# The first four projection units of layer 0 on unnormed x, two of them side by side

## What is computed

```python
def rms_norm(x, g):
    y = xf * lax.rsqrt(jnp.mean(xf * xf, axis=-1, keepdims=True) + NORM_EPS)
    return y * g

h = rms_norm(x, norm_g)
proj = jnp.einsum('bsd,de->bse', h, w_in) + b_in
(a_q, a_k, a_v, i_q, i_k, i_w, ...) = jnp.split(proj, offsets, axis=-1)
a_k = partial_rope(a_k, cos, sin);  i_q = partial_rope(i_q, ...);  i_k = partial_rope(i_k, ...)
logits = jnp.einsum('bqhd,bsd->bqhs', iqb, ik)                     # indexer
score = jnp.einsum('bqhs,bqh->bqs', jax.nn.relu(logits), iwb)      # then top 128 of each row
...
x = x + jnp.einsum('bsd,de->bse', merged, w_out)
```

## Time and profile before

| | before |
|---|---|
| median of 3 runs | 1283.41 us |
| the profiled execution's own time | 1283.52 us |
| its span (first to last instruction) | 1281.3 us |
| PE busy | 1263.1 us, 99% |
| DVE, ACT, POOL busy | 689.0, 633.3, 599.5 us |
| granted TensorE clock | 0.999 of full |

### The profile page before, as it was taken

The page is one execution under the profiler, slowest core; times in us unless marked ns, Lnnn a source line. Parts: engine busy times, 40 slices in busy tenths (PEclk is TensorE's granted clock), DMA queues, the critical chain, the costliest instruction groups (busy, mean ns, idle before and its releaser), DMA issues.

```text
span 1281.3 us, 19785 instructions
## 1 busy us (share of the span) xinstructions
PE 1263.1 (99%) x6486; PEld 1064.3 (83%) x6486; DVE 689.0 (54%) x1432; ACT 633.3 (49%) x1157; POOL 599.5 (47%) x759
## 2 busy tenths in 40 slices
PE   8999999999999999999999999999999999999997
PEld 6788888888988888888888888878888888888887
DVE  6799887745545221123687988785644631121144
ACT  6565676686534332333256466767754433323233
POOL 6654333423235555455775642333322455455463
PEclk9999999999999999999999999999999999999999
DMA  7223111221322323333342321122212222332331
GB/s 296 83 82 115 67 50 58 66 91 51 113 69 70 103 82 98 99 97 108 99 158 89 99 85 65 50 66 73 76 51 102 89 82 82 106 98 90 103 102 66
DMA packets 37047, 116.35 MB, mean 91 GB/s; under 512 B 4080, under 2 KB 4464, under 8 KB 36720
## 3 DMA queue, kind: packets, MB, share of 16 engines
q1 hardware_dynamic: 34672, 111.24, 26.3%
q10 hardware_dynamic: 2304, 4.20, 1.0%
HBM read 111.23 MB, written 4.19 MB: 90 GB/s over the span
## 4 chain that ended last, share of the span: by engine, by line
PE 92%; DVE 4%; ACT 2%; issue 1%; POOL 1%; DMA 0%; ACTq 0%; SPq 0%; DVEq 0%; POOLq 0%
PE acc L653 75%; PE ps_o L812 5%; PE ps_t L799 2%; PE ps_t L790 2%; PE ps_s L768 2%; PE ps_o L819 1%; PE ps_s L774 1%; DVE turn L1371 1%; DVE bk_lo_s L1351 1%; PE ps_s L757 1%; PE acc L686 1%; PE spare L750 1%; PE spare L831 1%; DVE prob L1392 0%; DMA xT<-x 0%
## 5 line engine op out<-in xcount | busy, mean ns | idle before, releaser
L604 POOL TENSOR_TENSOR w_lo<-w_raw,w_hi 128x256 fp32r<-128x256 f32 x744 | 586.0, 817 | 664.2 <-ACT w_hi L889 664.0
L653 PE MATMUL acc<-h_hi,w_hi 128*128 128x512 f32 x1120 | 447.6, 400 | 0.7 <-POOL h_lo L615 0.7
L653 PE MATMUL acc<-h_lo,w_hi 128*128 128x512 f32 x1120 | 438.8, 392 | 0.0
L653 PE MATMUL acc<-h_hi,w_lo 128*128 128x512 f32 x1120 | 292.6, 395 | 0.0
L889 ACT ACTIVATE w_hi<-w_raw 128x1024 fp32r<-128x1024 f32 (+1 forms) x210 | 202.0, 962 | 119.5 <-PE acc L653 90.8
L653 PEld LDWEIGHTS acc<-h_hi,w_hi 128*128 128x128 f32 x1120 | 210.7, 188 | 41.7 <-POOL h_lo L615 1.8
L653 PEld LDWEIGHTS acc<-h_lo,w_hi 128*128 128x128 f32 x1120 | 210.7, 188 | 39.4
L653 PEld LDWEIGHTS acc<-h_hi,w_lo 128*128 128x128 f32 x1120 | 205.6, 188 | 40.4
L1513 DVE SCALAR_TENSOR_TENSOR gated<-prob,acc 128x512 f32<-128x512 f32 x16 | 11.0, 688 | 246.7 <-PE acc L653 246.7
L1131 ACT ACTIVATE prob<-acc,par_half 128x512 f32<-128x512 f32 x48 | 33.1, 690 | 147.1 <-PE acc L653 147.1
L1078 ACT ACTIVATE prob<-prob,neg_max 128x128 f32<-128x128 f32 (+3 forms) x128 | 70.7, 553 | 9.2 <-DVE neg_max L1392 8.9
(11 more groups left out here) (274 smaller groups left out, 1823.0 us busy)
## 6 DMA issues: line engine op xcount, KB each, us to landing
w_raw<-w_full SPq DMA_DIRECT2D x162, 512.0 KB, 3.4
w_raw<-w_mix SPq DMA_DIRECT2D x48, 256.0 KB, 2.6
rel<-rel ACTq DMA_DIRECT2D x16, 256.0 KB, 2.9
xT<-x SPq DMA_DIRECT2D x4, 512.0 KB, 6.2
stage<-x_tok SPq DMA_DIRECT2D x4, 512.0 KB, 10.1
xT<-x SPq DMA_DIRECT2D x1, 2048.0 KB, 9.3
x_kept<-xT SPq DMA_DIRECT2D x1, 2048.0 KB, 9.0
xT<-x_kept SPq DMA_DIRECT2D x1, 2048.0 KB, 8.3
```

Of the source, the lines that this page charges most:

```text
L604: last = pool.tensor_tensor(w_lo[:, slot, part, :], w_raw[:, raw, part, :], w_hi[:, slot, part, :].bitcast(F32), ALU.subtract)
L653: last = pe.matmul(acc[slot][:, :], w[:, slot, k, :], x[:, k, :], start=(place == 0), stop=(place == 3 * nk - 1))
```

## The change

In layer 0 a fourth unit (a_k) runs on unnormed x, and DVE scales it in a step of its own, `scale_ak`, ahead of the first rotation. Units 0 and 1 are no longer computed one after the other: their first 16 passes are dealt in turns as the chunks of x arrive, so that weights 1 are loaded between the second and the third pair of chunks, and ACT takes their high part there. On ACT the square root and the parameter copies stand in front of the reading of unit 0. The parameters are loaded in front of the last token tile. POOL splits the weights of units 2 and 3 ahead of its first `h_lo`, and those of unit 4 ahead of its third. In both layers `turn_iw` moves from unit 6 into unit 7, ahead of `turn_v`.

```diff
+RAW_X = (4, 3)
@@ schedule(l)
     if l == 0:
-        seq.extend((("passes", (0, 0, PASSES)), ("squares", 0), ("read", 0), ("norm_sum", 0), ("high", 2)))
-        seq.extend((("passes", (1, 0, SPREAD)), ("norm_spread", 0), ("passes", (1, SPREAD, PASSES)), ("h", 0), ("h", 1), ("unit", 1)))
+        seq.extend((("passes", (0, 0, DC)), ("passes", (1, 0, DC))))
+        for k in range(DC, 2 * DC, 2):
+            seq.extend((("passes", (0, k, k + 2)), ("passes", (1, k, k + 2))))
+        seq.extend((("passes", (0, 2 * DC, PASSES)), ("squares", 0), ("norm_sum", 0), ("read", 0), ("high", 2)))
+        seq.extend((("passes", (1, 2 * DC, PASSES)), ("norm_spread", 0), ("unit", 1)))
         seq.append(("passes", (2, 0, PASSES)))
-        seq.extend(("h", c) for c in range(2, DC))
+        seq.extend(("h", c) for c in range(4))
         seq.append(("unit", 2))
+        seq.extend(("h", c) for c in range(4, DC))
...
     seq.extend((("passes", (3, 0, PASSES)), ("unit", 3)))
+    if l == 0:
+        seq.append(("scale_ak", 0))
     seq.extend(("rope", u) for u in range(XG_UNITS))
...
-    seq.append(("turn_iw", 0))
     seq.extend((("iq_hi", 1), ("ik_hi", 0), ("iq_lo", 0), ("iq_lo", 1), ("ik_lo", 0)))
     units(6, 7)
-    seq.append(("turn_v", U_AV))
+    seq.extend((("turn_iw", 0), CUT, ("turn_v", U_AV)))
     index(1)
@@ sync, layer 0
                     load(l, 0, 0, full(0), DC)
-                    for c in range(2, DC, 2):
-                        load_x(c)
+                    load_x(2)
                     load(l, 1, 1, full(1), DC)
+                    load_x(4)
+                    load_x(6)
...
+                    load_params()
                     load_tokens(3)
-                    load_params()
@@ gpsimd
-                for u in range(3):
+                done = 5 if l == 0 else 4
+                for u in range(done - 1):
                     split(l, u, u, DC)
                 for c in range(1, DC, 2):
-                    if c == (3 if l == 0 else 5):
-                        split(l, 3, 3, DC)
+                    if c == 5:
+                        split(l, done - 1, done - 1, DC)
                     pool.wait_ge(h_hi_ready, l * DC + c + 1)
                     pool.tensor_tensor(h_lo[:, c, :], h_full[c % 4], ...).then_inc(h_odd, 1)
@@ scalar, start
-                if c == 1:
-                    high_part(0, 0, 0, 0)
-            high_part(0, 0, 0, 1)
+                if c % 2 and c < 4:
+                    high_part(0, 0, 0, c // 2)
@@ scalar, read_sums
-                    if n < XG_UNITS:
+                    if n < RAW_X[l]:
-                        act.activation(iq[:, n, :] if n < U_IK else ik[:, :], src, ACT.Copy).then_inc(evac, 1)
+                        act.activation(iq[:, n, :] if n < U_IK else ik[:, :] if n == U_IK else ak[:, :], src, ACT.Copy).then_inc(evac, 1)
@@ vector
+                    elif kind == "scale_ak":
+                        dve.wait_ge(evac, evacs(l, U_AK))
+                        link(dve.tensor_tensor(ak[:, :], ak[:, :], spare[:, :], ALU.mult))
+                        link(dve.tensor_scalar(ak[:, :], ak[:, :], par[:, U_AK:U_AK + 1], None, ALU.add))
```

More of the change, by code:

```diff
@@ L64 @@
 K_ID, K_CHUNK, K_CAUSAL, K_COS, K_SIN, KCOLS, K_SEL = 0, 128, 256, 384, 896, 1408, 1408
-SPREAD = 16
 INDEX_AT = {U_AK + 7: 2, U_AK + 12: 3}
@@ L608, in _ @@
             for l in range(DEPTH):
-                for u in range(3):
+                done = 5 if l == 0 else 4
+                for u in range(done - 1):
                     split(l, u, u, DC)
                 for c in range(1, DC, 2):
-                    if c == (3 if l == 0 else 5):
-                        split(l, 3, 3, DC)
+                    if c == 5:
+                        split(l, done - 1, done - 1, DC)
                     pool.wait_ge(h_hi_ready, l * DC + c + 1)
                     pool.tensor_tensor(h_lo[:, c, :], h_full[c % 4], h_hi[:, c, :].bitcast(F32), ALU.subtract).then_inc(h_odd, 1)
-                with pool.Fori(0, (PROJ - 4) // RAW) as i:
-                    for b in range(4, RAW + 4):
+                with pool.Fori(0, (PROJ - done) // RAW) as i:
+                    for b in range(done, RAW + done):
                         split(l, i * RAW + b, b, DC)
-                for u in range(4 + (PROJ - 4) // RAW * RAW, PROJ):
+                for u in range(done + (PROJ - done) // RAW * RAW, PROJ):
                     split(l, u, u, DC)
@@ L728, in _ @@
                         n, first, to = n
-                        product(l, n, n, 0, h_hi if n >= XG_UNITS else xg_hi, h_lo if n >= XG_UNITS else xg_lo, DC, first, to,
+                        product(l, n, n, 0, h_hi if n >= RAW_X[l] else xg_hi, h_lo if n >= RAW_X[l] else xg_lo, DC, first, to,
                                 (lambda k: pe.wait_ge(xg_ready, l * DC + k + 1)) if n == 0 else
-                                (lambda k: pe.wait_ge((h_even, h_odd)[k % 2], l * (DC // 2) + k // 2 + 1)) if n == XG_UNITS else None)
+                                (lambda k: pe.wait_ge((h_even, h_odd)[k % 2], l * (DC // 2) + k // 2 + 1)) if n == RAW_X[l] else None)
                     elif kind == "norm_sum":
@@ L1249, in _ @@
             for l in range(DEPTH):
-                base[0] = l * DVE_STEPS + PRE
+                base[0] = l * (DVE_STEPS + 2)
                 count[0] = 0
@@ L1501, in _ @@
                             last.then_inc(normed, 1)
-                assert count[0] == DVE_STEPS, count[0]
+                assert count[0] == DVE_STEPS + (2 if l == 0 else 0), count[0]
                 hold(dve, "dve")
```

## The result

The changed kernel takes **1288.38 us** (1287.21 to 1288.64) against 1283.41 for the kernel before: a ratio of 1.0035, 95% interval 1.0026 to 1.0045. It is slower by 5.0 us, and above the range of the prediction (1282.6 to 1287.2). Its profiled execution took 1288.64 us (before 1283.52), with a span of 1286.7 (before 1281.3).

What follows compares the result with a forecast made beforehand. PE, busy 99% of the span, was taken as the bound. Terms -1.45 - 1.5 + 1.0 + 3.85 - 0.1 = +1.8 on the profiled 1283.52 gave 1285.3; with the median 0.11 lower, 1285.2 us, range 1282.6 to 1287.2.

Steps and rivals of the forecast that it cites:

- Loads, units 0 and 1: Start of layer 0: weights 1 land at 9.3, PE's stream holds from 11.48, unit 2 starts at 21.9, 1.45 us gained.
- lock-out for a whole GpSimd instruction: Chunks 4 to 7 beside POOL's split: 1.54 each, PE loses 1.5 more, 1286.7; 0.04 of rival 2's chance.
- Rival 3: Loads at the start don't land in issue order, weights 1 as late as before: +3.4, 1286.9; chance 0.06.
- Units 2 to 4: Unit 3's 1.5 of waiting goes, unit 4 loses about 1.0 waiting for `h_lo`; unit 5 starts at 39.4, 1.9 ahead.
- Start of the rotations: DVE in layer 0: after the h chain and `scale_ak`, the first rotation starts at 35.75 against 32.11.
- rival 2: POOL's slower splits delay `h_lo` 1 and DVE's chain; `iw` read at 57.4, +3.3 less 0.1, 1286.7; chance 0.24.
- I take 16.1, since POOL is idle at their end: DVE's three rotations in layer 0 take 16.1 us instead of 16.5, ending at 51.85.
- The low parts: DVE behind the rotations in layer 0: `iq_lo` falls from 3.24 to 2.4, `ik_lo` takes 1.38; `iw` done at 56.05.
- the lag goes to the end whole: Behind `turn_v`, which starts 1.9 late after a 4 us stand, index scores and scans keep their distances to the end.
- Layer 1: DVE does the low parts while formerly waiting 3.37 for `turn_iw`; PE gains 0.1 at the index score at most.

Runs made afterwards that it cites:

- Experiment 7: Changed kernel with GpSimd computing only a quarter of the low parts of the weights of units 5, 6 and 7 in layer 0: 1283.19 us.
- Experiments 1: Changed kernel with twenty passes into an unused score bank added in front of `turn_v` in layer 0: 1285.57 us.
- 3: Changed kernel, layer 0: DVE reads `iw` right behind the rotations; 7 unused passes before `turn_v`, 14 before the first index score: 1285.15 us.
- experiment 4: Kernel before the change, with only the move of `turn_iw` behind unit 6, in front of `turn_v`, in both layers: 1283.32 us.
- experiments 2: Changed kernel with DVE in layer 0 reading `iw` right behind the rotations, in front of `iq_lo`; PE's order unchanged: 1286.27 us.

## Why the prediction was wrong

The sign and the place were right, the size was not: +1.8 forecast, +5.0 measured. By its steps:

- **Loads, units 0 and 1.** Right. Weights 1 land at 2.66 + 6.6 = 9.3 us, as forecast. The stream runs from 11.55 (11.48 forecast) and chunk 7 is used at 16.28 (16.06 to 16.1). Beside the split a chunk took 4.74 / 4 = 1.19, inside 1.15 to 1.2. (The row at 28.24 behind that price lay beside a split for its first half only and then beside POOL's own `h_lo`; the price held all the same.) The Trainium skill's lock-out for a whole GpSimd instruction ("Who interferes with whom") would have made it 1.54, and the measurement decides against that. Unit 2 starts at 21.80 (21.9): 1.57 gained, 1.45 forecast. Rival 3 falls with it.
- **Units 2 to 4.** Right. Unit 4 starts at 33.00 (32.95) and unit 5 at 39.30 (39.4). The wait for `h_lo` is there, 0.86 in two pieces (6.30 for a unit of 5.44; 1.0 forecast).
- **Start of the rotations.** Right in the sum, 35.72 for 35.75, and partly by luck: the chain of h ended at 33.75, so that `scale_ak` could start some 0.4 earlier than forecast, and its addition took 1.14 where 0.5 to 0.86 were put down. `h_lo` 1 ended at 29.4 (29.5), so rival 2 in its own form (two slow splits ahead of it) did not happen, though its time for the reading of `iw`, 57.4, is nearly the measured one.
- **"I take 16.1, since POOL is idle at their end".** This is the first step that failed. The rotations took 17.7. I had looked only at their end, and there it came true: the last product with `turn` took 0.70 for 1.03. But the first one took 1.04 for 0.70, and so gave it back. And the splits moved by 3.4 us where these rotations moved by 3.8 to 4.2 (units 1 and 2). So three `TENSOR_SCALAR` instructions that had started in GpSimd's gaps, two of them only 0.2 to 0.3 ahead of a split, now lie beside one: all five take 4.27 for 3.10, which is the 17.67 - 16.49. Experiment 7 shows the cause by taking GpSimd away. The Trainium skill (SBUF — State Buffer, "Who interferes with whom", "Which ops grab the shared pair") names `tensor_scalar` among the instructions that can contend with GpSimd; the rows agree, 0.97 against 0.49. I had used that page for another step and not here. The low parts took 2.27 (2.4), and `iw` was released near 57.3 instead of 56.05, **+1.25**.
- **"the lag goes to the end whole".** The second step that failed, by leaving a term out. I counted a stand of PE at its length. TensorE's granted clock fell, and the eleven starts behind it were nearly twice as far apart: **+2.5**. Experiments 1 and 3 show it. I had read PE's distances only where PE hardly stood, and taken 0.23 a pass for all of it.
- **Layer 1.** 0.3 came back, 0.1 forecast.

With both put right the sum closes: 1.8 + 1.3 + 2.5 - 0.2 = 5.4, the difference of the spans; the profiled executions themselves differ by 5.1, since 0.3 less lies around the span of after.

What stays open: what decides in one execution whether the clock falls. In the profiles slow starts followed the stands of 2.15, 2.82, 3.26 and 5.17, and none the stands of 1.44, 1.99, 2.14 and 2.74; and experiment 4 shows them behind waits of 0.85, 0.41 and 0.41. So the length of the stand does not settle it. The times say that it differs from one execution to the next: in experiments 2 and 7, and in the changed kernel itself, where two of seven times are 1287.2 and 1287.3 with a mean clock of 0.997 and 0.996, and the others 1288.1 to 1288.6 with 0.995. No experiment varied the work in front of a stand.

## What to carry to other kernels

A gain at the front of the critical engine is worth what is left of it at the next place where that engine waits for another: compute when the other's chain gets there, with each instruction priced by what lies beside it at its new time, not its old one. If it will be late, move the request and not the work, and then look for the engine in between (here ACT) that stands for the late one in order. And a stand of TensorE is priced at its length and the slower passes behind it; if it can't be avoided, passes that nobody reads kept the clock in both kernels that had them.

## What was not expected of the hardware

- The granted clock fell from full to the lower level around four stands of PE from 2.15 to 5.17 us, in two of these profiles only when PE was back at work, and once behind waits of 0.85 and less; it held around other stands of up to 2.74. The starts were then 0.427 apart instead of 0.23, eleven of them after a stand of 5.17 and eight after one of 3.26. In both kernels that filled the stand with passes without a use, it did not fall there (1285.57 for 1288.38; a spread of 0.7 instead of 2.8).
- A VectorE `TENSOR_SCALAR` of 128x512 fp32 took 0.49 alone and 0.94 to 0.97 beside GpSimd's subtractions; one on 8 partitions 0.41 and 0.84, so it is not the number of partitions. The product with `consts` took 0.69 alone and 1.10 beside them, the sum with `ps_o` 0.69 both times.
- The shuffle behind a 4-partition `TENSOR_SCALAR` (`f_row`) started some 0.75 us after its end, with GpSimd beside it or without (at 45.34 in before, 50.47 in after, 46.85 in experiment 7).
